# Grouped attention: four of sixteen heads have their probabilities turned by VectorE instead of TensorE

## What is computed

```python
qkv = h @ w_qkv
q = apply_axial_rope(rms_norm_2(q, q_gain), cos, sin) * (HEAD_DIM ** -0.5)
k = apply_axial_rope(rms_norm_2(k, k_gain), cos, sin)
...
sc = jnp.einsum('bqkgd,bskd->bkgqs', q_blk, k).astype(jnp.float32)
p = jax.nn.softmax(sc, axis=-1).astype(v.dtype)
return jnp.einsum('bkgqs,bskd->bqkgd', p, v)
...
return o @ w_o
```

## Time and profile before

| what | value |
| --- | --- |
| median of 3 runs | 2992.82 us (2992.47 to 2994.85) |
| profiled execution, its own time | 2992.58 us |
| span in the profile | 2990.8 us |
| TensorE busy | 2980.2 us |
| VectorE busy | 1981.6 us |
| ScalarE busy | 1530.8 us |
| granted TensorE clock | 1.0 throughout |

### The profile page before, as it was taken

The page is one execution under the profiler, slowest core; times in us unless marked ns, Lnnn a source line. Parts: engine busy times, 40 slices in busy tenths (PEclk is TensorE's granted clock), DMA queues, the critical chain, the costliest instruction groups (busy, mean ns, idle before and its releaser), DMA issues.

```text
span 2990.8 us, 36930 instructions
## 1 busy us (share of the span) xinstructions
PE 2980.2 (100%) x13913; PEld 2491.5 (83%) x13913; DVE 1981.6 (66%) x2621; ACT 1530.8 (51%) x2098; POOL 297.2 (10%) x245
## 2 busy tenths in 40 slices
PE   9999999999999999999999999999999999999999
PEld 7888888988888888888888888888888888888887
DVE  6666668789578676666666655558876666666554
ACT  6656564555654664544444444467845444444443
POOL 0043200245000450000000000001000000000000
PEclk9999999999999999999999999999999999999999
DMA  9664345555455544655665555565456566655554
GB/s 343 216 225 156 122 148 175 176 183 170 141 168 191 176 154 142 193 189 192 196 194 185 194 199 194 186 201 178 141 197 195 188 194 196 193 185 195 200 194 143
DMA packets 256563, 553.90 MB, mean 185 GB/s; under 512 B 9808, under 2 KB 42720, under 8 KB 245696
## 3 DMA queue, kind: packets, MB, share of 16 engines
q1 hardware_dynamic: 255616, 550.82, 56.0%
q0 software_dynamic: 544, 1.48, 0.2%
q10 hardware_dynamic: 288, 0.07, 0.0%
HBM read 550.24 MB, written 2.10 MB: 185 GB/s over the span
## 4 chain that ended last, share of the span: by engine, by line
PE 98%; DVE 1%; ACT 0%; DMA 0%; issue 0%; ACTq 0%
PE psum L751 42%; PE psum L2521 32%; PE psum L2662 16%; PE psum L2798 2%; PE psum L1642 2%; PE psum L1620 1%; PE psum L1637 1%; PE psum L1593 1%; PE psum L2260 0%; PE psum L980 0%; DVE weights_lo L560 0%; PE psum L1851 0%; PE psum L2131 0%; PE psum L1645 0%; DMA shape_consts<-in_consts 0%; PE psum L1899 0%
## 5 line engine op out<-in xcount | busy, mean ns | idle before, releaser
L560 DVE TENSOR_TENSOR weights_lo<-weights,weights_hi 128x1024 fp32r<-128x1024 f32 (+2 forms) x1015 | 1261.6, 1252 | 713.0 <-ACT weights_hi L542 710.1
L542 ACT ACTIVATE weights_hi<-weights 128x1024 fp32r<-128x1024 f32 (+2 forms) x1015 | 1055.3, 1048 | 1253.2 <-PE psum L751 531.6
L751 PE MATMUL psum<-weights_hi,act_hi 128*128 128x512 f32 (+3 forms) x1952 | 762.8, 391 | 0.3 <-DVE weights_lo L560 0.2
L751 PE MATMUL psum<-weights_hi,act_lo 128*128 128x512 f32 (+3 forms) x1952 | 749.3, 384 | 0.0
L751 PE MATMUL psum<-weights_lo,act_hi 128*128 128x512 f32 (+3 forms) x1952 | 748.5, 383 | 0.0
L2521 PE MATMUL psum<-weights_hi,act_hi 128*128 128x512 f32 x1408 | 547.9, 389 | 0.0
L2521 PE MATMUL psum<-weights_hi,act_lo 128*128 128x512 f32 x1408 | 547.7, 389 | 0.0
L2521 PE MATMUL psum<-weights_lo,act_hi 128*128 128x512 f32 x1408 | 547.7, 389 | 0.0
L751 PEld LDWEIGHTS psum<-weights_hi,act_hi 128*128 128x128 f32 x1952 | 367.1, 188 | 69.2 <-issue 4.5
L751 PEld LDWEIGHTS psum<-weights_hi,act_lo 128*128 128x128 f32 x1952 | 366.7, 188 | 68.0
L751 PEld LDWEIGHTS psum<-weights_lo,act_hi 128*128 128x128 f32 x1952 | 367.3, 188 | 63.8
(11 more groups left out here) (256 smaller groups left out, 1953.2 us busy)
## 6 DMA issues: line engine op xcount, KB each, us to landing
weights<-in_ffn_w_gate SPq DMA_DIRECT2D x88, 1024.0 KB, 5.2
weights<-in_ffn_w_up SPq DMA_DIRECT2D x88, 1024.0 KB, 5.1
weights<-in_ffn_w_down SPq DMA_DIRECT2D x88, 1024.0 KB, 4.8
weights<-in_odd_w_in SPq DMA_DIRECT2D x40, 1024.0 KB, 5.1
weights<-in_even_w_in SPq DMA_DIRECT2D x36, 1024.0 KB, 5.1
weights<-in_w_out SPq DMA_DIRECT2D x32, 1024.0 KB, 5.0
weights<-in_rnn_w_in SPq DMA_DIRECT2D x32, 1024.0 KB, 5.5
weights<-in_attn_w_qkv SPq DMA_DIRECT2D x24, 1024.0 KB, 5.1
```

The source lines that it names most:

```text
L542: e.nc.scalar.activation(e.WH[(2 * slot + b) % HL][:, 0:n // 2], e.RAW[slot][:, b * n // 2:(b + 1) * n // 2], ACT.Copy).then_inc(self.hi.s ...
L560: e.nc.vector.tensor_tensor(e.WL[s][:, 0:n // 2], e.RAW[slot][:, b * n // 2:(b + 1) * n // 2], e.WH[s][:, 0:n // 2].bitcast(F32), ALU.subt ...
L751: last = e.nc.tensor.matmul(e.PS[:, banks.start + m, 0:w], a, x, start=(kk == 0 and n == 0), stop=(kk == KT - 1 and n == 2))
```

## The change

For heads 1, 4, 7 and 10 (`FLIPPED`) TensorE no longer turns E and ScalarE no longer copies the turned tiles. In their place VectorE, directly behind its multiplication of the head, issues sixteen block transposes (`flip`) that read 32 partitions by 2 by 2 by 32 elements of E and write the same to the kept piece, crossing from partition group r to partition group c. The last of them raises `pcopied`, after waiting until the head before has been copied. The exponentials of the next head wait for `pcopied` of this head, where they waited for `pturned`. The count of `pturned` leaves these heads out. `flips`, a `short` buffer and a general `flip` are added to the base class `Pairs`; the two other attention layers pass such a buffer, but no pair of theirs is marked, and their instructions are the same.

```diff
@@ class Pairs
+        self.short = [n for n, p in enumerate(pairs) if p.get("flipped")]
+        self.PTS = short
...
+    def flips(self, n):
+
+        return self.pturned.sem, self.pturned.at(n - len([k for k in self.short if k < n]))
...
-        if s - self.TURN in self.at:
+        if s - self.TURN in self.at and self.at[s - self.TURN] not in self.short:
             n = self.at[s - self.TURN]
             pe.wait_ge(*self.ready(n))
...
             act.wait_ge(self.negmax.sem, self.negmax.at(n + 1))
-            if n:
-
-                act.wait_ge(self.pturned.sem, self.pturned.at(n))
+            if n - 1 in self.short:
+
+                act.wait_ge(self.pcopied.sem, self.pcopied.at(n))
+            elif n:
+
+                act.wait_ge(*self.flips(n))
...
-        if s - 2 - self.TURN in self.at:
+        if s - 2 - self.TURN in self.at and self.at[s - 2 - self.TURN] not in self.short:
             n = self.at[s - 2 - self.TURN]
-            act.wait_ge(self.pturned.sem, self.pturned.at(n + 1))
+            act.wait_ge(*self.flips(n + 1))
             self.copy(act, n)
@@ class Gqa
+    FLIPPED = 1, 4, 7, 10
...
@@ Gqa.vector
             nc.vector.tensor_tensor(self.E, self.E, self.col(3, n).unsqueeze(2).to_broadcast([P, 2, T]), ALU.mult).then_inc(self.normed.sem, 1)
+            if n in self.short:
+                self.flip(dve, n)
+
+    def flip(self, dve, n):
+
+        dve.wait_ge(self.normed.sem, self.normed.at(n + 1))
+        src = self.E.rearrange("p i (k x) -> p i k x", k=MT)
+        dst = self.kept[n % 12].rearrange("p (k i x) -> p i k x", k=MT, i=2)
+        for r in range(4):
+            for c in range(4):
+                if r + c == 6:
+
+                    dve.wait_ge(self.pcopied.sem, self.pcopied.at(n))
+                ins = self.e.nc.vector.transpose(dst[32 * c:32 * c + 32, :, :, 32 * r:32 * r + 32], src[32 * r:32 * r + 32, :, :, 32 * c:32 * c + 32])
+        ins.then_inc(self.pcopied.sem, 1)
```

More of the change, by code:

```diff
@@ L1507, with __init__ @@
     TURN, VALUES, STATS = 1, 2, 304
-    def __init__(self, e, turns, pairs, E, PT):
+    def __init__(self, e, turns, pairs, E, PT, short=None):
         self.e, self.turns, self.pairs, self.E, self.PT = e, turns, pairs, E, PT
@@ L1525, in end @@
             s.advance(k)
-        for s in (e.s_score, e.s_negmax, e.s_clamped, e.s_inverse, e.s_pturned, e.s_pcopied, e.s_pv, e.s_stored):
+        e.s_pturned.advance(n - len(self.short))
+        for s in (e.s_score, e.s_negmax, e.s_clamped, e.s_inverse, e.s_pcopied, e.s_pv, e.s_stored):
             s.advance(n)
@@ L1562, in ready @@
         return self.exp.sem, self.exp.at(2 * n + 2)
+    def flips(self, n):
+        return self.pturned.sem, self.pturned.at(n - len([k for k in self.short if k < n]))
+    def flip(self, dve, n):
+        older = [k for k in self.short if k < n]
+        dve.wait_ge(self.exp.sem, self.exp.at(2 * n + 2))
+        if older:
+            dve.wait_ge(self.pv.sem, self.pv.at(older[-1] + 1))
+        for r in range(4):
+            for c in range(4):
+                if n and r + c == 6:
+                    dve.wait_ge(self.pcopied.sem, self.pcopied.at(n))
+                ins = self.e.nc.vector.transpose(self.PTS[32 * c:32 * c + 32, :, 32 * r:32 * r + 32], self.E[32 * r:32 * r + 32, :, 32 * c:32 * c + 32])
+        ins.then_inc(self.pcopied.sem, 1)
     def copy(self, act, n):
@@ L1619, in tensor @@
                 for kt in range(p["keys"] // P):
-                    last = nc.tensor.matmul(self.O(n)[:, i, :], self.PT[:, i, kt * P:(kt + 1) * P], p["v"][i][:, kt, :], start=(kt == 0),
+                    turned = self.PTS if n in self.short else self.PT
+                    last = nc.tensor.matmul(self.O(n)[:, i, :], turned[:, i, kt * P:(kt + 1) * P], p["v"][i][:, kt, :], start=(kt == 0),
                                             stop=(kt == p["keys"] // P - 1))
@@ L1709, in vector @@
             nc.vector.scalar_tensor_tensor(first, second, self.col(4, n)[:, 1:2], first, ALU.mult, ALU.add).then_inc(self.mixed.sem, 1)
+        if s - 2 in self.at and self.at[s - 2] in self.short:
+            self.flip(dve, self.at[s - 2])
     def sums_inverted(self, dve, n):
@@ L1782, in __init__ @@
         buffers = pr[:, :, c["kc"]:c["kc"] + 512].rearrange("p j (i k) -> p j i k", i=2)
-        super().__init__(e, turns, pairs, buffers[:, 0], buffers[:, 1])
+        super().__init__(e, turns, pairs, buffers[:, 0], buffers[:, 1], pr[:, 0, c["mz"]:c["mz"] + T].rearrange("p (i k) -> p i k", i=2))
         late = EVEN_CHUNKS[10][0]
@@ L2089, in __init__ @@
         buffers = pr[:, :, c["iq"]:c["iq"] + 512].rearrange("p j (i k) -> p j i k", i=2)
-        super().__init__(e, turns, pairs, buffers[:, 0], buffers[:, 1])
+        super().__init__(e, turns, pairs, buffers[:, 0], buffers[:, 1], pr[:, 0, c["iq"] + 512:c["iq"] + 512 + T].rearrange("p (i k) -> p i k", i=2))
         self.roped = self.heads.final(c["ik"])
@@ L2228, in __init__ @@
             pairs.append(dict(slot=self.SCORES + h, keys=T, q=[pr[:, m, h * DH:(h + 1) * DH] for m in range(MT)], k=[keys(k)] * 2, mask=None,
-                              scores=[self.turned(h * DH), self.turned(k0), self.turned(k0 + 256)], sum=None, factor=None))
+                              scores=[self.turned(h * DH), self.turned(k0), self.turned(k0 + 256)], sum=None, factor=None, flipped=h in self.FLIPPED))
         kept = (GQA_H + 2 * GQA_G) * DH
```

5 lines of the change are left out of this document (added).

## The result

The changed kernel takes 2999.91 us in the median of 14 launches (2998.31 to 3002.27), the kernel before 2993.59 in 14 on the same chip (2992.44 to 2997.68): a ratio of 1.0021, 95% interval 1.0014 to 1.0028. It is slower by 6.3 us, and the interval excludes 1. The forecast was 2996.0, range 2991.5 to 3003.5. Among the experiments one launch, of the kernel with half of the transposes, took 3730.13 us on a slower clock and is left out of its ratio.

What follows compares the result with a forecast made beforehand. TensorE was taken as the bound, busy for the whole span. Head terms 0.6 + 1.8 + 1.1 - 0.2 gave +3.3 us, a span of 2994.1 and a forecast of 2996.0 us, range 2991.5 to 3003.5.

Steps and rivals of the forecast that it cites:

- the first rival: VectorE's transposes cost by instruction, not element: 7.1 us a head, +11.7 us, 3004.3 us; chance 0.24.
- the second: Rival: transposes all hidden, TensorE's wait overestimated, so -1.7 us shows in full: 2991.1 us; chance 0.10.
- between +1.7 and +6: Change in us where most of the forecast's own 0.60 chance lay; +1.7 was its sum at 4.6 us a head.
- the third: Rival: GpSimd's later rotation of the next queries makes TensorE wait at heads 4 and 7: +6.1, 2998.7 us; chance 0.06.
- Head 1: TensorE waits 0.6 us before scores of head 3 and 0.4 before head 2's turn; net +0.6 us.
- -0.42: TensorE time in us saved by each removed turn, credited at heads 1, 4 and 7; four turns 1.7 us.
- Head 4: Query scaling follows the transposes; TensorE waits 1.4 us before head 6's scores, 0.8 before head 5's turn; net +1.8 us.
- Head 7: Delay of 3.1 us reaches head 9; TensorE waits 0.3, 0.5 and 0.8 us; net rounded to +1.1 us.
- The wait of 0.3: Term at head 7: TensorE waits 0.3 us for head 8, counted before it asks at 1103.3 us.
- Head 10: Transposes fill VectorE's 5.03 us idle hole before the output projection's first weight half; net -0.2 us.
- the late `act_lo`: Head 10: up to 0.5 us of delay may reach the first `act_lo`, which the fourth pair of values needs.
- The one-for-one rule: Each further us of a head's transposes costs 1 us more at each of heads 1, 4, 7 and 10.

Runs made afterwards that it cites:

- the kernel with half of the transposes: Against the kernel before: heads 1, 4, 7, 10 get a plain copy and eight of sixteen transposes, half the blocks unturned; 2993.92 us, ratio 1.0002.
- the copy kernel: Against the kernel before: turns of heads 1, 4, 7, 10 removed, one plain VectorE copy in place of the transposes, probabilities unturned; 2992.74 us, ratio 0.9994.
- the only-added kernel: Against the kernel before: 64 VectorE transposes added at heads 1, 4, 7, 10, TensorE's turns and ScalarE's copies kept; 3000.64 us, ratio 1.0025.
- fillers: The changed kernel plus TensorE products into an unused PSUM bank ahead of its waits; 3000.64 us, ratio 1.0025 to the kernel before.
- spare buffer: The changed kernel, but flipped heads' exponentials go to an unused kept piece, so the next head's need not wait for transposes; 3000.0 us, ratio 1.0021.
- head 4 only: Against the kernel before: only head 4 is flipped by VectorE; 2996.0 us, ratio 1.0011.
- heads 1 and 4: Against the kernel before: the change at heads 1 and 4 only; 2997.04 us, ratio 1.0011.
- behind the maxima: The spare-buffer kernel with all 16 transposes of a flipped head moved behind the next head's maxima, ahead of its sums; 3007.88 us, ratio 1.0045.

## Why the prediction was right in its mechanism and off in its size

**Right.** TensorE is the bound; a turn is worth 0.42 us where the next instruction is ready; a head's transposes take 5.05 us, not lengthened by GpSimd; the next head's maxima and sums are late by that and make TensorE wait at the places named; head 4 is the worst; the copies on ScalarE and the weight halves are hidden. Of the rivals' mechanisms the first is out (303 ns, not 444), the second is out, and GpSimd is named in no wait of TensorE. The size is another matter: +6.3 lies beyond the "between +1.7 and +6" where most of the forecast lay. The range holds it because its upper part had been opened for the first rival, which did not come, and so that is luck; 2998.7, worked out for the third, is nearer to 2999.9 than my 2996.0. TensorE stays the better place at these heads, which the Trainium skill advises (VectorE: DVE Perf Modes, Rules for kernel authors); the trace agrees, with 0.42 us for TensorE's turn of a head against 5.05 us for VectorE's.

**The sum was half of what came: +3.3 predicted, +6.9 in the stretch** (+6.4 in the span, since the heads began 0.5 us earlier). By its terms:

*Head 1*, +0.6 against +1.34. Two parts. The waits were 1.32 us and not 1.0, since the weight half behind the transposes took 1.79 us (1.2 assumed) while GpSimd ran. And a wait costs more than its idle time: -0.42 + 1.32 is 0.90, and 0.44 is missing. The prediction counted a stall as idle time alone, and this step failed: the scores' wait costs 0.16 above it, the turn's 0.28. The rows show what is missing. Weight products are listed with 0.39 us and start 0.23 apart, so neighbours overlap by 0.16; idle time is counted from the listed end and leaves this out. At the turn the same comes to 0.15 (scores of 1.02 us, turn 0.87 behind their start), and scores behind a wait are listed with 1.10 us, 0.08 more. So in the kernel after the turn of head 2 starts 1.27 us behind the scores with an idle time of 0.16; before it was 0.87. The last 0.05 are not resolved.

*Head 4*, +1.8 against 2.0 to 2.1 without a fall of the clock. The waits were 1.97 for 2.2 predicted, and the 0.46 above idle time make up for it. The fall of the clock, which no term held, adds 1.56 here, of which about half comes back at head 7.

*Head 7*, +1.1 against +1.33, or 2.09 where the clock held. The wait of 0.3 that I had given to the scores of head 9 is there only in the latter case, at 0.72. In the kernel after these scores are 0.08 us late and the turn behind them 0.17, too short to be listed as waits; the waits of the next head are 1.02 us, where 1.3 had been worked out.

*Head 10*, -0.2 against +0.69. Two steps failed. One is "-0.42": its turn stood ahead of the value products, where the copy kernel shows that removing it gives 0.04. The other is the late `act_lo`, which was seen and given "up to 0.5 us" but booked at some 0.2; it idles TensorE 0.49 us and costs 0.73. The first makes 0.38 of the difference, the second 0.51.

Together these make up the difference: 0.74 at head 1, 1.78 at head 4 (1.56 of it the clock), 0.23 at head 7 and 0.89 at head 10, 3.6 us. So the mechanism held and the sizes were off, above all the stall counted as idle time alone, the turn and the `act_lo` of head 10, and the clock. Seen from the other side, the turns give what they should at one place only: the only-added kernel costs 0.44 more at head 7 than the one with fillers (2.53 and 2.09), and the same at heads 1, 4 and 10.

The one-for-one rule of the prediction ("for each further us of a head's transposes ... 1 us more") was not tested above 5.05 us. Below it, the kernel with half of the transposes has 1.4 us less on VectorE per head (3.6 for 5.05): by the rule +6.2 - 5.8 = +0.4, measured -0.2.

**Open.** What makes the clock fall, and why at 210 us in some launches and at head 4 in others. Of 14 profiled executions six had the one at 210 us, with no wait of TensorE near it. Six have long unfilled waits at head 4: 1.41 and 0.56 us (after, spare buffer, head 4 only, heads 1 and 4), 1.06 and 0.56 (only added), 3.57 (behind the maxima). Three of them had the fall there (after, spare buffer, behind the maxima), and these are the three without one at 210 us. The launches without a profile tell only the mean clock: it was below 1.000 in 13 of 14 of the kernel after and in all 10 with the spare buffer, in 7 of 11 with fillers, and in 53 of 100 of the kernel before. So a low clock is more frequent with these waits, but where it fell in those launches is not on record. That is a pattern, not a cause shown.

## What to carry to other kernels

Moving work off the bounding engine brings its time back only where the next instruction there is ready; ahead of a wait, or of a stretch that the engine's own issue limits, it brings nothing. Price added work on another engine by what stands directly behind it in the queue: the same 5 us were free behind heads 2, 11, 14 and 15 and cost 1.3 to 2.1 us behind heads 1, 4 and 7. Count VectorE's idle time ahead of the next maxima and the slack behind the exponentials together: 6.2 us at head 2, 4.2 at head 1 and 3.7 at head 4. Add to every stall what it costs in overlap, here 0.16 to 0.28 us.

## What was not expected of the hardware

- TensorE's clock fell to 1.2 GHz for 3.4 us at the end of the second of two waits of 1.41 and 0.56 us, and did not fall at the same two in two other executions (head 4 only, heads 1 and 4). In the kernel with the transposes behind the maxima it fell while TensorE still stood in its wait of 3.57 us, and came back 6.8 us later.
- It also falls with TensorE busy: at 210 us, in or just behind 3.6 us of products with 15 columns (`128x15`), in six of 14 executions; the other eight have these products and no fall. In four of the six the heads begin 1.2 to 1.4 us later than before.
- A transpose of 32 x 128 elements took 299 to 309 ns in all 64 cases, and a head's sixteen 5.05 us both at head 1, with GpSimd running, and at head 4, with GpSimd idle. The two-input weight half took up to 1.79 us beside GpSimd instead of 1.22, and GpSimd's multiplication of 128 x 256 (L1404) up to 1.78 us beside such a half, where beside the transposes of head 1 it took 0.73 to 0.74.
- VectorE's plain copy of a head (128 x 512) took 568 ns; the sixteen block transposes of the same data 5.05 us, nine times that.
